# Hybrid decoder step: second half of the first expert gather moved behind the first unit, five extra wide products while the routing is worked out, counts in a bank of their own

## What is computed

```python
t = x.reshape(-1, D_MODEL)
g_prob = softmax(t @ w_rg + b_rg); g_idx = argmax(g_prob)          # 1 of 4 groups
e_logits = (t @ w_re + b_re) of that group                          # 8 experts in a group
top_v, top_i = lax.top_k(softmax(e_logits), 2)                      # 2 of 8 experts
comb = group weight * normalised top_v, per token and expert
for g in range(MOE_GROUPS):
    hg = silu(t @ w_gate[g]) * (t @ w_up[g])                        # 32 experts, D_FF = 512
    out = out + (hg * comb) @ w_down[g]
```

## Time and profile before

| | us |
|---|---|
| median of 3 runs | 1175.29 |
| lowest, highest | 1173.21, 1176.48 |
| the profiled execution | 1177.6 |
| its span, first to last instruction | 1175.9 |
| TensorE busy | 1004.2 (85%) |
| VectorE busy | 460.2 (39%) |
| mean granted TensorE clock | 0.916 |
| HBM traffic | 297 MB, 252 GB/s over the span |

### The profile page before, as it was taken

The page is one execution under the profiler, slowest core; times in us unless marked ns, Lnnn a source line. Parts: engine busy times, 40 slices in busy tenths (PEclk is TensorE's granted clock), DMA queues, the critical chain, the costliest instruction groups (busy, mean ns, idle before and its releaser), DMA issues.

```text
span 1175.9 us, 15998 instructions
## 1 busy us (share of the span) xinstructions
PE 1004.2 (85%) x6653; PEld 677.7 (58%) x6653; DVE 460.2 (39%) x782; ACT 302.9 (26%) x601; POOL 53.2 (5%) x77
## 2 busy tenths in 40 slices
PE   3999999999999999999898979768786777677574
PEld 2778567986669999989867854323231323232121
DVE  3998956304667454545454331010101020101014
ACT  4042124225436434534433340000000000000001
POOL 1602300001110000000000000000000000000000
PEclk9999999999999999999999969988788878798778
DMA  9482433003536384523678427999999999999993
GB/s 274 100 201 74 159 124 138 7 37 87 187 101 233 123 305 146 189 73 132 209 289 327 173 108 302 421 422 421 421 420 421 421 421 422 421 421 422 421 418 139
DMA packets 91267, 297.70 MB, mean 253 GB/s; under 512 B 21037, under 2 KB 30985, under 8 KB 67004
## 3 DMA queue, kind: packets, MB, share of 16 engines
q1 hardware_dynamic: 88420, 288.25, 64.2%
q0 software_dynamic: 2256, 7.80, 1.9%
q10 hardware_dynamic: 520, 0.62, 0.2%
HBM read 286.76 MB, written 9.90 MB: 252 GB/s over the span
## 4 chain that ended last, share of the span: by engine, by line
PE 39%; DMA 17%; SPq 16%; DVE 3%; issue 1%; ACT 1%; DVEq 0%; ACTq 0%
SPq L580 14%; DMA ring<-in_w_exp_down_dram 9%; PE bank L1568 5%; PE bank L1570 5%; PE bank L1569 5%; PE bank L1844 3%; PE bank L1222 3%; DMA ring<-in_w_exp_up_dram 2%; DMA ring<-in_w_exp_gate_dram 2%; PE bank L1861 2%; PE bank L1579 2%; PE bank L1875 2%; PE bank L1581 2%; PE bank L1580 2%; PE bank L1494 2%; DMA work<-in_w_exp_down_dram 2%
## 5 line engine op out<-in xcount | busy, mean ns | idle before, releaser
L1844 PE MATMUL bank<-ring,work 128*32 128x512 f32 x768 | 143.4, 715 | 28.2 <-DMA work<-in_w_exp_gate_dram 14.6
L1237 PE MATMUL bank<-work,ring 128*128 128x320 f32 (+1 forms) x496 | 132.1, 425 | 0.5 <-DVE work L1973 0.5
L1844 PE MATMUL bank<-work 128*32 128x512 f32 x256 | 110.3, 706 | 22.0 <-DMA ring<-in_w_exp_gate_dram 14.7
L1568 PE MATMUL bank<-ops,usplit 128*128 128x320 f32 x368 | 114.1, 310 | 1.1 <-DVE usplit L2266 1.1
L1569 PE MATMUL bank<-ops,usplit 128*128 128x320 f32 x368 | 113.9, 310 | 0.0
L1570 PE MATMUL bank<-ops,usplit 128*128 128x320 f32 x368 | 113.9, 309 | 0.0
L1237 PEld LDWEIGHTS bank<-work,ring 128*128 128x128 f32 x496 | 94.2, 193 | 33.4 <-issue 2.4
L1861 PE MATMUL bank<-ring,work 128*32 128x512 f32 x384 | 88.8, 852 | 27.0 <-DMA work<-in_w_exp_down_dram 14.8
L1861 PE MATMUL bank<-work 128*32 128x512 f32 x128 | 67.8, 875 | 36.2 <-DMA ring<-in_w_exp_down_dram 36.2
L2266 DVE TENSOR_TENSOR usplit<-ring,usplit 128x2048 fp32r<-128x2048 f32 x32 | 73.3, 2292 | 61.8 <-ACT usplit L945 61.5
L1844 PEld LDWEIGHTS bank<-ring,work 128*32 128x32 f32 x768 | 34.7, 128 | 74.3 <-issue 71.4
(11 more groups left out here) (435 smaller groups left out, 1528.5 us busy)
## 6 DMA issues: line engine op xcount, KB each, us to landing
ring<-in_w_exp_up_dram SPq DMA_DIRECT2D x50, 1024.0 KB, 26.7
ring<-in_w_exp_gate_dram SPq DMA_DIRECT2D x46, 1024.0 KB, 27.0
ring<-in_w_exp_down_dram SPq DMA_DIRECT2D x45, 1024.0 KB, 26.8
ring<-in_w_in_dram SPq DMA_DIRECT2D x11, 2048.0 KB, 9.1
work<-in_w_exp_gate_dram SPq DMA_DIRECT2D x18, 1024.0 KB, 26.4
work<-in_w_exp_down_dram SPq DMA_DIRECT2D x15, 1024.0 KB, 26.5
work<-in_w_exp_up_dram SPq DMA_DIRECT2D x14, 1024.0 KB, 26.7
ring<-in_w_glu_dram SPq DMA_DIRECT2D x4, 2048.0 KB, 8.4
```

Source lines behind the costliest of these rows:

```text
L1237: ins = nc.tensor.matmul(b[:, 0:N], wv[:, k, P * (m % 4):P * (m % 4 + 1)], src[:, k, 0:N], start=(k == 0), stop=(k == KT - 1))
L1568: nc.tensor.matmul(b[:, 0:T], wh, hi_[:, k], start=(k == 0), stop=False)
L1844: ins = nc.tensor.matmul(psum[part][ES * x:ES * (x + 1), :], xs[i % 2][:, kk, x], wt[x][:, k], start=(kk == 0), stop=(kk == KT - 1))
```

## The change

Three edits. (1) The second half of the first gather, X0.1, leaves LEAD and stands behind the first unit, U0, of the first group; ahead of it TensorE waits for `npass`. (2) After taking the bank of "rk" and ahead of the wait for rt_m, TensorE does five products of 128x512 into PSUM bank 7, whose result is read by nobody. (3) The counts leave the list of jobs and the six banks in turn: they go to bank 7, and VectorE waits for a semaphore of their own, `nm`. TensorE's wait for free banks ahead of the loop then ends with that of "rk".

```diff
--- before.py
+++ after.py
@@ -61,12 +61,13 @@
     if i:
         x["E1"] = [f"T{i}"] + [f"S{i - 1}.{k}" for k in range(2 * NC)]
     else:
+        x["U0"] = ["X0.1"]
         x["U3"].append("T0")
     return x
 
 
 EXTRA = [phase_extras(i) for i in range(NQ)] + [{}]
-LEAD = ["X0.0", "X0.1"]
+LEAD = ["X0.0"]
 TRAIL = [f"S{NQ - 1}.{k}" for k in range(2 * NC)]
 SIDE = LEAD + [e for x in EXTRA for c in PHASE for e in x.get(c, ())] + TRAIL
 SB = (4, 5, 6, 7)
@@ -178,7 +179,7 @@
         j += [f"o{u}{c}" for c in range(NC - (u == 3))]
         if u:
             j += [f"ft{2 * u - 2}", f"ft{2 * u - 1}"]
-    j += [f"o3{NC - 1}", "ft6", "ft7", "lg", "rk", "nm"]
+    j += [f"o3{NC - 1}", "ft6", "ft7", "lg", "rk"]
     return j
 
 PLAN = plan()
@@ -199,7 +200,7 @@
 
     "zs dtx sp_e dt_ready cs_in wdec etot bblk zf ze csm mt y_done ysq yr yn glu_used "
 
-    "whi wlo hn_hi hn_lo yb_hi yb_lo u5_hi u5_lo mrg_hi mrg_lo q_hi q_lo ao_hi ao_lo diag rsb ssq rsn tn wrg nmax prn nmax_s pexp_s sb_full ob_full osb zeroed lgT rt_lg rt_a rt_e rt_m rt_d rt_x window npass "
+    "whi wlo hn_hi hn_lo yb_hi yb_lo u5_hi u5_lo mrg_hi mrg_lo q_hi q_lo ao_hi ao_lo diag rsb ssq rsn tn wrg nmax prn nmax_s pexp_s sb_full ob_full osb zeroed lgT rt_lg nm rt_a rt_e rt_m rt_d rt_x window npass "
 
     "raw_rest unit_done half_done sil hid sel selw side4 side5 side6 side7 got4 got5 got6 got7 y_a y_b pass_done fy "
 
@@ -1791,6 +1792,9 @@
                 ins = tr(b[0:R, 64 * c:64 * c + NG + NG * NE], lgT[0:NG + NG * NE, P * c:P * c + R], NG + NG * NE)
             end(ins, "lg")
             b = take("rk")
+
+            for _ in range(5):
+                nc.tensor.matmul(psum[7][:, :], ones[:, :], tT[:, 0:2].rearrange("p k t -> p (k t)")[:, 0:BLK], start=True, stop=True)
             pe.wait_ge(s["rt_m"], 1)
             nx = NG * NE
             nc.tensor.matmul(b[:, 0:NC * nx], before[:, :], moh[:, :, NG:], start=True, stop=False)
@@ -1798,11 +1802,10 @@
                 ins = nc.tensor.matmul(b[:, nx * (c + 1):NC * nx], ones[:, :],
                                        moh[:, c:c + 1, NG:].to_broadcast([P, NC - 1 - c, nx]), start=False, stop=(c == NC - 2))
             end(ins, "rk")
-            b = take("nm")
             for c in range(NC):
                 R = ROWS[c]
-                ins = nc.tensor.matmul(b[:, 0:nx], ones[0:R, :], moh[0:R, c, NG:], start=(c == 0), stop=(c == NC - 1))
-            end(ins, "nm")
+                ins = nc.tensor.matmul(psum[7][:, 0:nx], ones[0:R, :], moh[0:R, c, NG:], start=(c == 0), stop=(c == NC - 1))
+            ins.then_inc(s["nm"], 1)
             assert at[0] == len(PLAN)
 
             for i in range(RB):
@@ -1914,6 +1917,8 @@
                             gate_up(i, int(c[1]))
                         elif c[0] == "E" and i:
                             down(i - 1, int(c[1]))
+                        if i == 0 and c == "U0":
+                            pe.wait_ge(s["npass"], 1)
                         for item in EXTRA[i].get(c, ()):
                             side_work(item)
                 read_passes(pe, npass)
@@ -2519,9 +2524,8 @@
             q(TT(rt[:, 18], rt[:, 18], rt[:, 10], ALU.add))
             q(TT(comb[:, :, :], rt[:, 18], wide(top(16), NE), ALU.mult))
 
-            got(dve, "nm")
-            emptied(dve.reduce_max(rt[:, 20, 0, 0:1], bank("nm")[:, 0:NG * NE], AX.X), "nm")
-            done(dve, "nm")
+            dve.wait_ge(s["nm"], 1)
+            q(dve.reduce_max(rt[:, 20, 0, 0:1], psum[7][:, 0:NG * NE], AX.X))
             q(TT(win[:, 0:9], win[:, 0:9], rt[:, 20, 0, 0:1].to_broadcast([P, 9]), ALU.is_lt))
             q(dve.tensor_reduce(rt[:, 21, 0, 0:1], win[:, 0:9], AX.X, ALU.add))
             TS(np_i[:, :], rt[:, 21, 0, 0:1], 1.0, None, ALU.add).then_inc(s["npass"], 1)
```

## The result

The changed kernel takes 1170.5 us (median of 20 runs) against 1176.4 us for the kernel before: ratio 0.9945, 95% interval 0.9935 to 0.9955, a gain of 6.5 us (5.3 to 7.6); one execution of the kernel before, 1240.4 us, lies far off the rest and is left out of the ratio. I had forecast 1165 us, a gain of 10.1, with a range from 1160.5 to 1169.0: 1170.5 lies above it. The direction holds, and so does the path (the end of U0 starts the flow of weights); the size does not. 1.1 us of the miss is that the kernel before has a median of 1176.4 over 20 runs, where the three runs that I started from had 1175.3; the rest is in the gain. The profiled execution of the changed kernel took 1171.53 us, its span is 1169.8 us.

What follows compares the result with a forecast made beforehand. The end of U0, which starts the saturated weight flow, was taken to bound the kernel: 688.85 + 5.9 + 1.35 + 6.06 = 702.1 us, a gain of 10.1, so 1165 us on the 1175.3 median; range 1160.5 to 1169.0.

Steps and rivals of the forecast that it cites:

- the place of the clock's fall: First half of the first gather: one fall between ranks and its end, taken halfway, 5.9 us (bounds 4.3 and 7.5).
- the 438 us of weights taken as unchanged: Behind the first unit: 184.5 MB of expert loads at 421 GB/s, which nothing on an engine can shorten.
- the profile that it all started from: Baseline: the gain was summed on one execution of 1177.6 us, then applied to the median of 1175.3 us.
- U0 sets the end: Start of the weight flow: the first unit's end, 712.21 us, sets the kernel's end microsecond for microsecond.
- Counts in their own bank: Ahead of the gather: the selection releases it, 1.4 us earlier at 1.2 GHz, 2.35 us at 2.4 GHz.
- The second half behind U0: First gather: 24 of 48 records leave the path, 7.5 us at 1.2 GHz; ScalarE's bare evacuation adds 1.35 us.
- The queue does not run dry: Between first and second unit: second ends 8.8 us after first, under 9.9; contrary rival 1172.1 us, chance 0.06.
- the sign of being wrong that the prediction named: Flow of weights: the forecast would be wrong if its 438 us took longer than before.
- one fall partway: Between ranks and the end of the gather's first half the clock falls once: gain 10.1 us, chance 0.52.
- the wide products don't help: Rival: clock falls before the gather's first half, only reordering and bank count; gain 7.5 us, 1167.8 us, chance 0.16.
- The rule of the Trainium skill that I weighed: Rival: the gather's first half itself brings the clock back before the first unit; gain 10 us, 1165.3 us, chance 0.04.

Runs made afterwards that it cites:

- e4: The kernel before with the counts in their own bank and nothing else: 1175.0 us, ratio 0.9992.
- f4: Kernel before, second unit-waiting group of four loads held until the second expert group's first gather half: 443.04 us from seventeenth load's issue to last landing.
- f5: Kernel before, second unit-waiting group of four loads held until the third unit is done: 444.43 us from seventeenth load's issue to last landing.
- g1: The changed kernel with 136 increments of an unused semaphore at the start of TensorE's program: 1177.9 us.
- g2: f2 with 136 increments of an unused semaphore at the start of TensorE's program: 1174.8 us, ratio 0.9991.
- h1: f2 with 70 increments of an unused semaphore at the start of TensorE's program: 1167.7 us, ratio 0.9926.
- e1: The changed kernel without the five wide products: 1171.5 us, ratio 0.995.
- e2: The kernel before with the five wide products alone: 1175.5 us, ratio 0.9991.
- f2: The changed kernel with six wide products instead of five, one more behind the counts and one behind the gather's first half: 1165.5 us, ratio 0.9903.
- f3: The changed kernel with six wide products instead of five and one more behind the counts: 1166.1 us, ratio 0.9907.

## Why the prediction was wrong

Three terms of the sum were mis-sized: the place of the clock's fall (4), the 438 us of weights taken as unchanged (5), and the profile that it all started from (6). Point by point, in the order of its steps:

1. **U0 sets the end.** Right but for what B and C add. In all 18 profiles B lies between 443.0 and 444.5 us whatever A is, and A from 17 to 31 us. SyncE's longest wait behind the sixteenth load fell from 33.9 to 25.4 us.
2. **Counts in their own bank.** Right: released by the selection, 7.26 us behind the transposes (forecast 7.37). Worth 1.5 us in the profile of e4; too little for the runs to show by itself.
3. **The second half behind U0.** Right in kind. ScalarE's bare evacuation costs 1.54 us, not 1.35: it takes 1.14 itself, so the two handoffs are 0.2 us each. npass is no wait at all.
4. **Where the clock falls: the step that failed.** I took a fall halfway, X0.0 at 5.9 us, a middle between two bounds with no row behind it; it comes 0.4 to 0.6 us behind the gather's start in three of four profiles, and X0.0 takes 7.1 to 7.2 us, 1.2 us more than I took. U0 took 6.3 us, not 6.06. With the 0.2 us of step 3 this makes 8.5 us of A out of the forecast 10.1.
5. **"The queue does not run dry", and B taken as constant.** The first is right (U1 ended 8.65 us behind U0; forecast 8.8), the second was wrong by about 1.1 us (1.2 between the two profiles of the sum): one of sixteen parts lands late beside a fetch of instructions. f4 and f5 show that late feeding isn't it, g1, g2 and h1 that the place of the fetches is; that it is the last fetch is read from the packet records and not separated by a run. It was not among my rivals, since I had not looked at what else the DMA engines carry. But it is the sign of being wrong that the prediction named: the weights took longer than before.
6. **The profile as its own baseline.** The profile before had the latest rise of the clock of four with that seam (A 30.80, against 29.19, 29.20 and 29.88; mean 29.77). Summed against one execution, the gain was overstated by 1.0 us. I carried it over to the median as if the difference of 2.3 us between execution and median lay elsewhere.

8.5 - 1.2 - 1.0 = 6.3 us, against 6.5 measured (5.3 to 7.6). That the two agree so closely is partly luck: the second measurement of the changed kernel gave 8.1 us, A and B come from single executions, and C alone differs by 2.6 us between the three profiles of the changed kernel.

The forecast case, one fall partway, was the right case with the wrong place. In A alone the 8.5 us lie between it (10.1) and the rival "the wide products don't help" (7.5); the measured time, 1170.5 us, lies above both (1165 and 1167.8), as both took B as constant and started from the same profile. That rival is nearly what happened: against e1 the five products buy 1.5 us of A and 0.6 us in the runs. The rule of the Trainium skill that I weighed ("TensorE: Matmul & The Clock Gate", "What's actually happening": activity releases the throttle) doesn't hold for gather products at 1.2 GHz: in e2 TensorE is busy 14.53 of 15 us with them at a granted clock of 0.50. But once the clock is at 2.4 GHz it stays there through the same products, as f2 shows.

**A version that beats both:** f2. Three times on three sets of runs: 0.9903, 0.9918, 0.9895 of the kernel before, 10 to 12 us; and 1165.5 against 1169.4 us for the changed kernel on the same chip. f3, with one wide product fewer, can't be told from it (1166.1 us). f2 does for the clock what the change began: every stretch of the seam has wide work in it. Its three profiles all have the fall in C, which costs 1.5 to 1.7 us; wide work there was not tried.

## What to carry to other kernels

Where the end of a kernel is a saturated flow of DMA, look for what starts the flow; there a microsecond is a microsecond. Filler products were worth little here as long as a thin stretch stood between them and the work that they were meant for, and some 5 us of A once that stretch was filled too. Sum against several executions, or cut the profile at landmarks: a clock that steps at its own moments makes one execution a baseline that is off by a microsecond. And when a flow is saturated on all DMA engines, look at what else they carry, near its end above all: instructions too.

## What was not expected of the hardware

- A fetch of TensorE's instructions (16 KB) takes 1.0 to 1.1 us of one DMA engine, and there are 54 in this kernel. Where the last one within the flow of 443 us begins at 441.6 to 442.3 us, one of the last sixteen parts lands about 1.1 us late (B 444.1 to 444.4 instead of 443.0 to 443.3); where it begins at 441.1 us or earlier, none does (f5, with its hole, apart).
- 136 increments of a semaphore by TensorE took 21.8 us, 0.16 us each.
- Behind the last landing the granted clock stayed at 1.00 in nine profiles and fell in nine; the rest of the kernel took 20.4 to 20.5 us in the first and 21.8 to 23.0 us in the second.
- Four loads of 1 MiB under way kept the DMA queue full for a group issued 7.7 us (f4) and 8.65 us (the changed kernel) behind them; at 11.3 us (f5) there was a hole, and it cost 1.3 us.
